# A 64-row, 32 by 32 fp32 product in front of each run of main products, on one Trainium2 core

## What is computed

```python
for i in range(DEPTH):
    hn = rmsnorm_2(h, ln_mix[i])
    ...
    h = h + mixed @ w_out[i]
    h = h + memory_cross_attention(rmsnorm_2(h, ln_x[i]), rmsnorm_2(mem, ln_mem[i]), ...)
    hn = rmsnorm_2(h, ln_mlp[i])
    h = h + jnp.square(jax.nn.relu(hn @ mlp_w1[i])) @ mlp_w2[i]
```

## Time and profile before

| what | value |
|---|---|
| time, median of 3 runs | 2944.84 us (2943.95 to 2947.85) |
| time of the profiled execution | 2946.84 us |
| its span, first to last instruction | 2945.0 us |
| PE, PEld busy | 2830.4 us (96%), 2519.4 us (86%) |
| DVE, ACT busy | 1999.5 us (68%), 1504.9 us (51%) |
| mean granted clock of PE | 0.988 of full speed |

### The profile page before, as it was taken

The page is one execution under the profiler, slowest core; times in us unless marked ns, Lnnn a source line. Parts: engine busy times, 40 slices in busy tenths (PEclk is TensorE's granted clock), DMA queues, the critical chain, the costliest instruction groups (busy, mean ns, idle before and its releaser), DMA issues. The chain is left out here.

```text
span 2945.0 us, 44951 instructions
## 1 busy us (share of the span) xinstructions
PE 2830.4 (96%) x18499; PEld 2519.4 (86%) x18499; DVE 1999.5 (68%) x1985; ACT 1504.9 (51%) x1445; POOL 66.0 (2%) x56
## 2 busy tenths in 40 slices
PE   7999999899999999999999999999999899999999
PEld 6799998788888888888886778999899888999898
DVE  6655565588888888888886656566555665665554
ACT  3443454467677667676773426444433336443442
POOL 1000000000000000000000210000000110000000
PEclk9999999899999999999999999999999999999999
DMA  6255540599999999999996333444355343444453
GB/s 191 72 184 187 175 152 22 194 372 329 370 332 345 356 330 369 331 352 348 335 366 204 136 107 98 149 162 144 109 188 186 127 129 103 149 150 130 134 190 106
DMA packets 365129, 619.48 MB, mean 210 GB/s; under 512 B 14664, under 2 KB 201126, under 8 KB 363700
## 3 DMA queue, kind: packets, MB, share of 16 engines
q1 hardware_dynamic: 363432, 611.77, 60.6%
q10 hardware_dynamic: 1550, 5.57, 0.5%
HBM read 611.93 MB, written 5.37 MB: 210 GB/s over the span
## 5 line engine op out<-in xcount | busy, mean ns | idle before, releaser
L365 DVE TENSOR_TENSOR slots_low<-slots,w_hi 128x2048 fp32r<-128x2048 f32 x240 | 550.2, 2296 | 385.3 <-ACT w_hi L354 384.8
L354 ACT ACTIVATE w_hi<-slots 128x2048 fp32r<-128x2048 f32 x240 | 452.5, 1889 | 334.7 <-PE ps L948 179.1
L1293 DVE TENSOR_TENSOR slots_low<-slots,w_hi 128x2048 fp32r<-128x2048 f32 x224 | 504.2, 2286 | 68.8 <-ACT w_hi L1241 68.8
L467 PE MATMUL ps<-x_hi,w_hi 128*128 128x256 f32 x1520 | 435.8, 287 | 31.6 <-DVE x_lo_low L552 15.5
L467 PE MATMUL ps<-x_lo_low,w_hi 128*128 128x256 f32 x1520 | 428.5, 282 | 0.0
L467 PE MATMUL ps<-x_hi,slots_low 128*128 128x256 f32 x1520 | 428.3, 282 | 0.0
L1241 ACT ACTIVATE w_hi<-slots 128x2048 fp32r<-128x2048 f32 x224 | 416.9, 1908 | 1.0 <-DMA slots<-in_moe_w_up_dram 0.8
L1173 PE MATMUL ps<-slots_low,x_hi 128*128 128x512 f32 x896 | 349.7, 390 | 0.0
L467 PEld LDWEIGHTS ps<-x_hi,w_hi 128*128 128x128 f32 x1520 | 292.3, 192 | 38.7 <-issue 30.5
L467 PEld LDWEIGHTS ps<-x_hi,slots_low 128*128 128x128 f32 x1520 | 292.7, 193 | 0.0
L467 PEld LDWEIGHTS ps<-x_lo_low,w_hi 128*128 128x128 f32 x1520 | 292.3, 192 | 0.3
(11 more groups left out here) (519 smaller groups left out, 5362.9 us busy)
## 6 DMA issues: line engine op xcount, KB each, us to landing
slots<-in_moe_w_gate_dram SPq DMA_DIRECT2D x112, 1024.0 KB, 5.1
slots<-in_moe_w_up_dram SPq DMA_DIRECT2D x112, 1024.0 KB, 5.1
slots<-in_moe_w_down_dram SPq DMA_DIRECT2D x112, 1024.0 KB, 4.9
slots<-in_mlp_w_dram SPq DMA_DIRECT2D x64, 1024.0 KB, 5.3
slots<-in_w_in_dram SPq DMA_DIRECT2D x54, 1024.0 KB, 5.3
slots<-in_ffn_w_gate_dram SPq DMA_DIRECT2D x14, 1024.0 KB, 4.9
slots<-in_ffn_w_up_dram SPq DMA_DIRECT2D x14, 1024.0 KB, 5.0
slots<-in_ffn_w_down_dram SPq DMA_DIRECT2D x14, 1024.0 KB, 4.9
```

What stands on the lines that cost most here:

```text
L354: act.activation(w_hi[:, s.buffer, 0:s.kt * s.cols], slots[:, s.slot, 0:s.kt * s.cols], ACT.Copy).then_inc(w_hi_done, 1)
L365: dve.tensor_tensor(slots_low[:, s.slot, 0:n], slots[:, s.slot, 0:n], w_hi[:, s.buffer, 0:n].bitcast(F32), ALU.subtract).then_inc(w_lo_don ...
L467: mm = pe.matmul(b[:, t * T:(t + 1) * T], w, xx[:, k, :], **flags)
L1293: dve.tensor_tensor(low[i % NS], raw[i % NS], his[i % R].bitcast(F32), ALU.subtract).then_inc(lo_done, 1)
```

## The change

`half_rows` is new: a single fp32 product of a 64-row, 32-column piece of `ones` with itself into a 32 by 32 corner of a bank that is about to be overwritten. In `linear` it is issued before the first part of item j, if j is 0, if item j-1 had a PE hook, if j is one of the items 1 to nn that follow a batch of squares (nn is the number of batches), or if j follows the transposed roots. In `mlp` it is issued before step 1, before the first down step, and in the last MLP before the first-steps among steps 5 to 8. In a stage whose source is split on the fly PE waits for the first chunk of the source before it.

```diff
@@ linear, on PE
                                 pe.wait_ge(act_emptied if e == "act" else dve_emptied, by[e].index(p - NB) + 1)
+                            if number == 0 and (j == 0 or ("pe", j - 1) in hooks or 1 <= j <= nn or j == turned_after + 1):
+                                if src.split and id(src) not in seen:
+                                    pe.wait_ge(src_lo_done, first_chunk[id(src)] + 1)
+                                half_rows(pe, p % NB)
                             tiles = what if kind == "fm" else range(TT)
@@ new
+        def half_rows(pe, b):
+
+            pe.matmul(bank(b)[0:32, 0:32], ones[0:64, 0:32], ones[0:64, 0:32], start=True, stop=True)
@@ mlp, on PE
                         wh, wl = split_weights(pe, slabs[i])
+                        if i == 1 or (store and 5 <= i <= 8 and kind == "first"):
+                            half_rows(pe, 4 + F * (g % 2) + n)
+                        if kind == "down" and g == 0:
+                            half_rows(pe, 4)
                         if kind == "first":
```

## The result

The changed kernel took 2960.2, 2961.1, 2971.1 and 2974.0 us. The ratio to the kernel before is **1.0058, with a 95% interval of 1.0039 to 1.0078: slower** by more than the prediction's 0.2%. (A disturbed run of 4761 us is left out.) The profiled execution is the one of 2974.01 us, its span 27.2 us longer than in the earlier trace rows.

A forecast was written before the change was run, and what follows sets the result against it. PE, busy for 96% of the span, was taken as the bound. 20.2 us paid, 24.1 us gained and some 0.4 us for settling gave -3.5 us: 2941.3 us against the median of 2944.84, range 2932 to 2955 us.

The forecast's parts named there:

- What sets it?: PE: work before a sequence sets pace; 33 of 47 slow behind 128-row work, 15 of 16 quick behind few-row products.
- with 15 of 16 sequences turned quick: 24.1 us: MLPs and linear stages: 5832 slow main products times 4.4 ns give 25.7 us, 24.1 us at that share.
- Two paces, 4.4 ns apart: Main products on PE run at 117.8 or some 113 ns at one clock; a quick one saves 4.4 ns.
- set at the start and kept: A sequence's pace is set at its start and stays until side work or a pause; 203.30 us stayed slow throughout.
- 64 rows in front give the quick pace: A 64-row product before every sequence lets main products start from an empty array and run quick, 4.4 ns less each.
- My 16 groups of few rows: Groups of fp32 products of 64, 33 or 8 rows on PE; 15 of 16 sequences behind them were quick.
- The exception: The one few-row fp32 group of 16 with a slow sequence behind it, 117.8 ns a product.
- the rival built on it: Long sequences of the first two MLPs enter slow, losing 13.7 of 25.7 us: 2953 us, slower; chance 16%.
- The other rivals: Main weights load ahead while the small product drains: 2936.0 us, 30%; pace doesn't come from the start: 2965 us, 8%.
- The price: 87 issues: 48 between full-array work at 0.34 us (16.3 us), 26 at 0.15 (3.9 us), 13 hidden; total 20.2 us.
- The noise: Some 2 us from lower-clock stretches, such as one at 2728.40 us costing about 1.6 us.
- my third rival: Pace of main products doesn't come from a sequence's start, so only 20.2 us of cost is left: 2965 us; 8%.

The follow-up runs named there:

- The second profile: The changed kernel unchanged, executed once more for another profile; it took 2961.85 us.
- run 25: Not a label but part of "run 25 times": the kernel before, unchanged, executed 25 times beside an experiment, between 2938.9 and 2960.7 us.

## Why the prediction was wrong

The sign was wrong: -3.5 us against some +15 to +27. The step that failed is *"What sets it?"*, with the term that hangs on it, *"with 15 of 16 sequences turned quick: 24.1 us"*.

- **Two paces, 4.4 ns apart: right; set at the start and kept: right for the long ones.** Over long sequences the spacing is 113.33 and 117.78 ns in every profile, and the 1776 products never changed over. But it can change without side work: in the run with the whole array at all sites, two sequences of 144 ran 48 products at the slow pace and, after one step of 123 or 124 ns, where the work passes from L476 to L471, the rest at the quick one.
- **64 rows in front give the quick pace: wrong.** Of the 6168 products in sequences that were slow before and got a small product, 2040 turned quick (8.2 us) and 4128 didn't; 744 that were quick turned slow (3.0 us). With 128 rows in the small product as many sequences were quick, 61 of 86 against 60, so the rows are not what decides. My 16 groups of few rows had more in common than their rows: 12 of them end in products of 128 columns, and none is followed by main products that load the data. Sorted by what stands ahead of the small product, the changed kernel's starts read: 256 or more columns 5 of 23 quick, up to 128 columns or main products 25 of 29, few-row groups 15 of 16, pauses 15 of 18. The second profile has 3 of 22, 27 of 30, 15 of 16 and 16 of 18. And of 12 sequences at L476, one was quick in either. A comparison of starts with a drain against starts without one had mixed all of these. And the rule was drawn from one execution. Nine profiles have the linear stages of the kernel before; of the 75 sequences there 23 were quick in all nine, 20 slow in all nine, and 32 came out either way. The sequences behind the twelve groups of 64 rows and 128 columns were always quick, but the run with two such sites alone shows that a product of that shape doesn't bring the pace along.
- **The exception was a hint, and no more.** It was the one group of my 16 with 64 rows, a 64 by 64 tile and 256 moving columns. The sequence behind it was quick in four of the nine profiles with that code, and quick in the changed kernel. I gave the rival built on it 16%. What it said came true in both MLPs, 13.7 us of the gain lost, but that it was this exception's doing is not shown. It gave 2953 us, because it left the linear stages' gain and my price standing.
- **The other rivals.** The main load does not go ahead of a 64-row product: 0.22 us from the first to the second main one at the sites shown, and 0.37 us a site. And the pace does depend on the start, only not on the rows in it: a product in front of the down sequences changed it.
- **The price: the drain was there, its size was low by 4.2 us.** 51 sites without a pause or a few-row group cost 18.0 us, 43 of them 0.37 each and the eight behind one-column products 0.26; I had 48 at 0.34 and thought 13 hidden. Behind few rows it was 0.17 (I had 0.15), and the 19 behind a pause or wait cost 0.19 each, so little of it was hidden. What I missed in the reading of the earlier trace rows is that an fp32 product stands as two loads and two product records there as well: the x8 are four products, and the small one has a second pass that my sum left out.
- **What the drain comes from: not asked.** I took it for the rows. 128 rows by 32 columns drain just so.
- **The noise: too small.** I allowed 2 us for the clock. The mLSTM cell stage alone makes 8.7, in three of 14 profiles, sequences change sides, and the kernel before, run 25 times beside an experiment, lay between 2938.9 and 2960.7 us.

Not settled: what in the start decides. The profiles show that short full-array products at all sites were followed by the quick pace 73 times of 86, that the work ahead of the small product and what the main products load go with the pace, and that some sequences change sides between two executions of one kernel. The mechanism was not isolated: no run changed the work ahead alone, or what is loaded alone. Whether the linear stages' longest sequences, 144 to 240 products, would pay for a full-array product of their own was not tried alone.

## What to carry to other kernels

Before a rule is built on "starts behind A are quick, starts behind B are slow", profile the same kernel twice and leave out what changes sides; then change one property at a time. A small product with the same 32 columns but 128 rows had as many quick starts and the same price, so neither belonged to the rows. Put a fix only where a long sequence pays for it: four sites of 0.22 us in front of some 3300 products gained 0.5%, while 87 sites with the same product broke even and with the draining one lost 0.6%. At 0.22 us a site in front of 48 products can't pay: 48 x 4.4 ns = 0.21 us.

## What the runs showed of the hardware that was not expected

- The same products on the same operands at a granted clock of 1.00 have two stable spacings, 113.33 and 117.78 ns. A single short product in front moved 1776 of them from one to the other. The Trainium skill ("TensorE: Matmul & The Clock Gate", section "Back-to-back issue gap") lists 262 cycles for 256 columns as the gap of products by themselves, and for loads and products in turn it has figures for 128 and 512 columns alone. Neither pace here is that gap (272 and 283 cycles at 2.4 GHz), and as the gap is not one for loads and products in turn, it did not bear on my third rival as I used it.
- A weight tile of 128 rows and 32 columns drains the array like one of 64 rows: behind products of 256 or 512 columns, 0.31 us in front of it in both, against 0.22 for the whole array.
- A short full-array product in fp32 costs 0.22 us in a stream, though its own two passes start only 28 to 33 ns apart behind products of 128 columns and more; in bf16, with one pass, it costs 0.11.
- The mLSTM cell stage runs at the upper or at the lower level of the clock from one execution to the next, 10.6 or 19.2 us, with the same kernel.
